# Three ring slots of the down stage loaded and split during the last quad, and two large reads cut into 256 KB pieces

## The reference

```python
def swiglu(h, w_gu, w_down):
    g, u = jnp.split(h @ w_gu, 2, axis=-1)
    return (jax.nn.silu(g) * u) @ w_down

x = x + MACARON_WEIGHT * swiglu(rms_norm(x, ffn1_norm[i]), ffn1_w_gu[i], ffn1_w_down[i])
...
x = x + MACARON_WEIGHT * swiglu(rms_norm(x, ffn2_norm[i]), ffn2_w_gu[i], ffn2_w_down[i])
gate = jax.nn.sigmoid(rms_norm(x, ple_norm[i]) @ ple_w_gate[i] + ple_b_gate[i])
e = rms_norm(p[i] @ ple_w_proj[i], ple_post_norm[i])
x = x + gate * e
```

## Time and profile before

| | us |
|---|---|
| median of three runs | 1810.19 (1809.73 to 1810.88) |
| the profiled execution, its own time | 1808.18 |
| its span, first to last instruction | 1806.1 |
| TensorE busy in it | 1706.2 (94%) |
| VectorE busy | 1290.5 (71%) |
| ScalarE busy | 694.9 (38%) |
| GpSimd busy | 296.0 (16%) |

### The profile page before, as it was taken

One profiled execution on the slowest core, in us unless ns is written; L12 is line 12 of the kernel. 1 busy time (PEld: TensorE's weight loads), 2 busy tenths in 40 slices (PEclk: granted clock), 3 DMA queues, 4 the chain that ended last, 5 costly groups with the idle time before them and its releaser, 6 DMA issues.

```text
span 1806.1 us, 20425 instructions
## 1 busy us (share of the span) xinstructions
PE 1706.2 (94%) x7314; PEld 1380.2 (76%) x7314; DVE 1290.5 (71%) x1812; ACT 694.9 (38%) x1120; POOL 296.0 (16%) x292
## 2 busy tenths in 40 slices
PE   7689999999988999999999889999999988999998
PEld 4478888888877888777777668888888866878877
DVE  7988676776644758678877799677667753666786
ACT  4343232232234435446644443223232223534442
POOL 6802221112200000024230001212221120000000
PEclk9889999999999999999899989999999989999999
DMA  7215444354377666121123214444444358776433
GB/s 280 82 43 208 169 145 166 143 181 144 125 270 254 213 217 191 57 80 47 36 76 117 82 64 146 169 154 167 163 152 158 122 181 297 226 234 189 152 121 127
DMA packets 122752, 277.69 MB, mean 154 GB/s; under 512 B 9723, under 2 KB 51356, under 8 KB 113948
## 3 DMA queue, kind: packets, MB, share of 16 engines
q1 hardware_dynamic: 115356, 263.02, 43.1%
q10 hardware_dynamic: 7296, 13.37, 2.1%
HBM read 198.23 MB, written 78.12 MB: 153 GB/s over the span
## 4 chain that ended last, share of the span: by engine, by line
PE 77%; DVE 14%; ACT 4%; issue 2%; DMA 2%; SPq 0%; ACTq 0%; DVEq 0%
PE bank L772 25%; PE bank L773 25%; PE bank L774 25%; DVE qb L1778 1%; DVE hn L1393 1%; DMA d_f<-in_wd 1%; PE bank L994 1%; DVE acc L1381 1%; ACT probs L1317 1%; DVE w_lo L1608 1%; DVE x_sb L1413 1%; DVE probs L1790 1%; DVE dn_lo L1661 1%; DVE h_lo L1425 1%; DVE rstd L1386 1%
## 5 line engine op out<-in xcount | busy, mean ns | idle before, releaser
L731 POOL TENSOR_TENSOR wdr<-wdr 128x256 f32<-128x256 f32 x176 | 165.3, 939 | 775.3 <-DMA wdr<-in_wd 765.0
L1661 DVE TENSOR_TENSOR dn_lo<-d_f,dn_hi 128x1024 fp32r<-128x1024 f32 x154 | 186.1, 1223 | 148.3 <-ACT dn_hi L1143 147.6
L772 PE MATMUL bank<-h_hi,t_hi 128*128 128x512 f32 x704 | 279.1, 396 | 6.4 <-DVE h_lo L1425 6.4
L773 PE MATMUL bank<-h_lo,t_hi 128*128 128x512 f32 x704 | 276.4, 393 | 0.0
L774 PE MATMUL bank<-h_hi,t_lo 128*128 128x512 f32 x704 | 276.0, 392 | 0.0
L772 PE MATMUL bank<-dn_hi 128*128 128x512 f32 x616 | 244.7, 397 | 29.7 <-DVE dn_lo L1661 13.9
L773 PE MATMUL bank<-dn_lo,dn_hi 128*128 128x512 f32 x616 | 242.5, 394 | 0.0
L774 PE MATMUL bank<-dn_hi,dn_lo 128*128 128x512 f32 x616 | 242.2, 393 | 0.0
L1143 ACT ACTIVATE dn_hi<-d_f 128x1024 fp32r<-128x1024 f32 x154 | 160.5, 1057 | 196.8 <-DMA d_f<-in_wd 116.7
L772 PE MATMUL bank<-c_hi,t_hi 128*128 128x512 f32 x528 | 205.4, 389 | 0.0
L773 PE MATMUL bank<-c_lo,t_hi 128*128 128x512 f32 x528 | 205.4, 389 | 0.0
(11 more groups left out here) (165 smaller groups left out, 2600.7 us busy)
## 6 DMA issues: line engine op xcount, KB each, us to landing
raw<-in_gu SPq DMA_DIRECT2D x44, 1024.0 KB, 5.7
actc<-acts SPq DMA_DIRECT2D x22, 1792.0 KB, 6.7
d_f<-actc SPq DMA_DIRECT2D x154, 256.0 KB, 3.0
raw_m<-in_units SPq DMA_DIRECT2D x52, 512.0 KB, 4.1
wdr<-in_wd SPq DMA_DIRECT2D x44, 512.0 KB, 5.4
wdc<-wdr SPq DMA_DIRECT2D x44, 512.0 KB, 3.4
d_f<-wdc SPq DMA_DIRECT2D x88, 256.0 KB, 3.2
d_f<-in_wd SPq DMA_DIRECT2D x66, 256.0 KB, 4.2
```

The source lines that it names most:

```text
L731: pool.tensor_tensor(blocks[to], blocks[one], blocks[two], ALU.add).then_inc(wd_made, 1)
L772: pe.matmul(ps, whi, vhi, start=first, stop=False, skip_group_check=onto)
L773: pe.matmul(ps, whi, vlo, start=False, stop=False, skip_group_check=onto)
L1661: dve.tensor_tensor(dn_lo[slot][:, :], d_f[slot][:, :], plain(dn_hi[slot][:, :]), ALU.subtract).then_inc(dn_split, 1)
```

## The change

Ring loads 0 to 3 move in SyncE's queue to the beginning of the last quad's round, ring load 4 between its `wd_load` and `wd_store`, and ring load 5 takes the place of ring load 2. ScalarE rounds steps 0 to 2 (`EARLY = 3`) behind `copy_p1` of the last quad, and VectorE splits them between `make_c22` and `make_c21`. The four reads of x become 16 of 256 KB, one behind each of the ring loads 12 to 27; the semaphores of x then count four pieces. The read of the per-layer input becomes eight of 256 KB, one behind each of the ring loads 45 to 52.

```diff
@@ -93,6 +93,8 @@
 STEPS = PRODUCTS * FH
 RING = 6
 STEP_INC = FH + 3
+
+EARLY = 3
 WD_AT = {P1: 0, P2: 2, Q3: 3}
 WDC_AT = {Q5: 0, Q7: 1, Q4: 2, Q6: 3}
 N_WD = 2 * FH
@@ -574,11 +576,10 @@
                 sp.dma_start(d_f[slot][:, HALF:2 * HALF].rearrange("p (h n) -> p h n", h=2),
                              weights.rearrange("h p n -> p h n")).then_inc(t2_in[slot], 16)
 
-            def x_reload(ph, i):
-                a, k = i // 2, (i % 2) * KH
+            def x_reload(ph, n):
+                a, k = n // KT, n % KT
                 src = xT if ph == 0 else x1
-                sp.dma_start(x_sb[:, k:k + KH, tok(a)],
-                             src[k * P:(k + KH) * P, tok(a)].rearrange("(k p) t -> p k t", p=P)).then_inc(x_back[i], 16)
+                sp.dma_start(x_sb[:, k, tok(a)], src[k * P:(k + 1) * P, tok(a)]).then_inc(x_back[n // KH], 16)
 
             def ffn(ph, first_units):
                 for q in (0, 1):
@@ -586,28 +587,32 @@
                     sp.wait_ge(done, value)
                     quad_load(ph, q + 2)
                 for q in range(1, QUADS):
+                    if q == QUADS - 1:
+
+                        for i in range(4):
+                            ring_load(ph, i)
                     if q % 2 == 0:
                         act_store(ph, q // 2 - 1)
                     wd_load(ph, q - 1)
+                    if q == QUADS - 1:
+                        ring_load(ph, 4)
                     wd_store(ph, q - 1)
                     if q + 3 < QUADS:
                         sp.wait_ge(t_split, t_count(ph, GU_AT[(q + 1, Q3)]))
                         quad_load(ph, q + 3)
-                ring_load(ph, 0)
-                ring_load(ph, 1)
                 wd_load(ph, N_WD - 1)
-                ring_load(ph, 2)
+                ring_load(ph, 5)
                 wd_store(ph, N_WD - 1)
-                for i in range(3, STEPS):
+                for i in range(RING, STEPS):
                     if i == RING + 1:
                         act_store(ph, FH - 1)
                     if i == FH + 1:
                         sp.wait_ge(wd_out, 16 * (ph + 1) * N_WD)
                         sp.wait_ge(act_out, 16 * (ph + 1) * FH)
                         sp.wait_ge(act_made, (ph + 1) * 2 * QUADS)
-                        for j in range(4):
-                            x_reload(ph, j)
                     ring_load(ph, i)
+                    if FH < i <= FH + 2 * KT:
+                        x_reload(ph, i - FH - 1)
                     if i >= FH + 4 and (i - FH - 4) % 4 == 0 and first_units:
                         if len(first_units) >= SLOTS:
                             sp.wait_ge(gu_made, (ph + 1) * NGU)
@@ -622,11 +627,13 @@
                         else:
                             for j in range(4):
                                 sp.wait_ge(e_out[j], 16 * (2 * KT // 4))
-                            sp.dma_start(e_sb[0][:, :, :], e_dram[0, :, 0:KT, :]).then_inc(e_in[0], 16)
                             for a in (0, 1):
                                 sp.wait_ge(re_out[a], 16)
                             sp.wait_ge(act_made, 4 * QUADS)
                             sp.dma_start(re_sb[0][:, :], e_dram[0, :, KT, :]).then_inc(re_in[0], 16)
+                    if ph == 1 and 4 * FH < i <= 4 * FH + KT:
+                        d = i - 4 * FH - 1
+                        sp.dma_start(e_sb[0][:, d, :], e_dram[0, :, d, :]).then_inc(e_in[0], 16)
 
             sp.dma_start(rel_sb[0:N_BUCKETS, :], rel).then_inc(rel_in, 16)
             sp.dma_start(oh_sb[:, :], onehot).then_inc(oh_in, 16)
@@ -1123,6 +1130,14 @@
                 act.wait_ge(c21_made, ph * QUADS + q + 1)
                 act.activation(w3[q % 2][:, :], w3[q % 2][:, :], ACT.Silu).then_inc(g1_made, 1)
 
+            def ring_round(ph, i):
+                slot, use = i % RING, ring_use(ph, i)
+                if i >= RING:
+                    act.wait_ge(dn_made, step_done(ph, i - RING))
+                act.wait_ge(s2_in[slot], 16 * use)
+                act.wait_ge(t2_in[slot], 16 * use)
+                act.activation(dn_hi[slot][:, :], d_f[slot][:, :], ACT.Copy).then_inc(dn_rounded, 1)
+
             def round_unit(n):
                 hi, _, size = unit_slot(n)
                 if slot_free(n):
@@ -1133,14 +1148,8 @@
             def down(ph):
                 na, nb = 4 * ph + 2, 4 * ph + 3
                 r = res_base(ph)
-                for i in range(STEPS):
-                    slot = i % RING
-                    if i >= RING:
-                        act.wait_ge(dn_made, step_done(ph, i - RING))
-                    use = ring_use(ph, i)
-                    act.wait_ge(s2_in[slot], 16 * use)
-                    act.wait_ge(t2_in[slot], 16 * use)
-                    act.activation(dn_hi[slot][:, :], d_f[slot][:, :], ACT.Copy).then_inc(dn_rounded, 1)
+                for i in range(EARLY, STEPS):
+                    ring_round(ph, i)
                     j, e = i // FH, i % FH
                     if j == J[P2] and e == 1:
                         for d in range(KH):
@@ -1202,6 +1211,9 @@
                     if q + 1 < QUADS:
                         for s in LOS1:
                             round_t(ph, GU_AT[(q + 1, s)])
+                    else:
+                        for i in range(EARLY):
+                            ring_round(ph, i)
                     gate0(ph, q)
                     gate1(ph, q)
                 down(ph)
@@ -1593,12 +1605,20 @@
                 make_c22(ph, q)
                 for n in todo[3:7]:
                     split_t(ph, n)
+                if not more:
+                    for i in range(EARLY):
+                        ring_split(ph, i)
                 make_c21(ph, q)
                 make_c12(ph, q)
                 gated(ph, q)
                 if q % 2:
                     mix_acts(ph, q // 2)
 
+            def ring_split(ph, i):
+                slot = i % RING
+                dve.wait_ge(dn_rounded, ph * STEPS + i + 1)
+                dve.tensor_tensor(dn_lo[slot][:, :], d_f[slot][:, :], plain(dn_hi[slot][:, :]), ALU.subtract).then_inc(dn_split, 1)
+
             def half_add(x, term, sign=1.0):
                 return dve.scalar_tensor_tensor(x, term, sign * MACARON_WEIGHT, x, ALU.mult, ALU.add)
 
@@ -1615,7 +1635,7 @@
 
                 def post_p2(d):
                     dve.wait_ge(dn_made, dn_count(ph, J[P2], FH - 1, d))
-                    dve.wait_ge(x_back[0], 16 * (ph + 1))
+                    dve.wait_ge(x_back[0], 16 * KH * (ph + 1))
                     half_add(out_tile(0, 0, d), bank2_of(P2, d)[:, :]).then_inc(res_added, 1)
 
                 def post_q6(d, i):
@@ -1626,7 +1646,7 @@
                         dve.tensor_tensor(w, bank2_of(Q6, d)[:, :], w, ALU.subtract).then_inc(w2d_made, 1)
                         return
                     dve.wait_ge(w2d_made, ph * KH + d + 1)
-                    dve.wait_ge(x_back[i], 16 * (ph + 1))
+                    dve.wait_ge(x_back[i], 16 * KH * (ph + 1))
                     a, h = [(0, 1), (1, 0), (1, 1)][i - 1]
                     sign = -1.0 if (a, h) == (1, 0) else 1.0
                     half_add(out_tile(a, h, d), w, sign).then_inc(x_step, 1)
@@ -1655,10 +1675,8 @@
                     dve.wait_ge(x_step, xs_q7(ph, d))
                     half_add(out_tile(1, 0, d), bank2_of(Q4, d)[:, :]).then_inc(res_added, 1)
 
-                for i in range(STEPS):
-                    slot = i % RING
-                    dve.wait_ge(dn_rounded, ph * STEPS + i + 1)
-                    dve.tensor_tensor(dn_lo[slot][:, :], d_f[slot][:, :], plain(dn_hi[slot][:, :]), ALU.subtract).then_inc(dn_split, 1)
+                for i in range(EARLY, STEPS):
+                    ring_split(ph, i)
                     j, e = i // FH, i % FH
                     if j == J[Q6]:
                         if e == 2:
@@ -1844,7 +1862,7 @@
                     dve.wait_ge(re_in[a], 16)
                     dve.reciprocal(re_sb[a][:, :], re_sb[a][:, :]).then_inc(e_rstd, 1)
                     dve.wait_ge(e_rstd, a + 1)
-                    dve.wait_ge(e_in[a], 16)
+                    dve.wait_ge(e_in[a], 16 * (KT, 1)[a])
                 link(dve.scalar_tensor_tensor(e, e, col(C_G["post"] + d), re_sb[a][:, :], ALU.mult, ALU.mult))
                 dve.wait_ge(sig_made, m + 1)
                 link(dve.tensor_tensor(e, e, sig[m % 2][:, :], ALU.mult))
```

## The result

The changed kernel takes 1786.38 us (median of four runs, 1782.53 to 1789.44), the kernel before 1810.54 on the same chip: a ratio of 0.9866 (95% interval 0.9854 to 0.9879), 24 us faster. Forecast were 1773.0 and a range of 1769.5 to 1781. The profiled execution is the slowest of the four, 1789.44 us.

A forecast was written before the change was run, and what follows sets the result against it. TensorE was taken as the bound nearly everywhere. 1808.2 less 37.5 us of removed stalls gave 1770.7, 1771.0 with 0.3 for step 7, and 1773.0 against the median; range 1769.5 to 1781.

The forecast's parts named there:

- The five terms of the gain: Stalls removed: early loads and splits 8.3 and 9.9 us, x in pieces 8.0 and 8.75, per-layer input 2.6; together 37.5.
- ScalarE's and VectorE's early work: Last quad: roundings of 3.2 us inside 10.28 idle, splits of 3.7 inside 4.75 idle; cost nothing.
- Step 3: Down stage: its split, still behind the mixes, has 1.9 and 1.2 us to spare; cost zero.
- the DMAs of steps 12 to 27: Down stage: ring loads, x pieces and units need 337 GB/s against 397 seen; queue 85% full, cost zero.
- SyncE's queue: Around the down stage's start: reordered loads and stores still serve steps 6 and 7 in time; 0.3 us in all.
- the term for steps 6 and 7: Start of both down stages: step 7 has 1.6 and 0.8 us to spare; 0.3 us taken in all.
- rival A: Down stage: step 3 or 7 misses TensorE beyond its spare; +5 or +10 us, time 1775 to 1783; chance 0.15.
- B: Steps 12 to 27 saturate DMA, noticed by TensorE from about 268 GB/s down; 1777 to 1793 us; chance 0.08.
- C: Small DMAs of steps 12 to 27 and 45 to 52 cost the queue fixed time; 1870 us; chance 0.03.
- D: Last quad: ring loads 0 to 3 stay late and the first split stays where it is; 1791 us; chance 0.04.

The follow-up runs named there:

- both_moves: Changed kernel with load 20 of the down weights ahead of ring loads 0 to 3 and last store of weight sums behind ring load 7; 1769.32 us.
- pieces_only: Kernel before with only the pieces of x and of the per-layer input, none of the early loads and splits; 1788.84 us.
- store_mid: Changed kernel with the last store of weight sums behind ring load 6, ahead of the store of activations and ring load 7; 1786.51 us.

## Why the prediction was wrong

**Right.** The five terms of the gain, 37.5 us. With the new waits taken out, a profiled execution took 1770.89 us (`both_moves`) against 1808.18, 37.3 less. They are right part by part too: the terms say 16.3 us for the first block and 21.25 for the second with the per-layer input, and the table shows 16.6 (735.2 to 718.6) and 21.4 (232.3 to 210.9). By medians `both_moves` gains 41.6 us, 4 more than the terms, and lies 3.7 us under the forecast of 1773.0: the two profiled executions lie 2.8 us under and 1.6 us over the medians they belong to, and no run tells why. ScalarE's and VectorE's early work fits into the idle time, though VectorE's with less room than costed: its three splits took 4.58 us and not 3.7, beside POOL's sums, and end 0.26 us before `make_c21` begins (504.89). Step 3 is in time, and the DMAs of steps 12 to 27 hold up nobody: the rates of 256 KB ring loads carried over to the pieces. On this the Trainium skill's rule of at least 1 MiB a DMA ("DMA: Bandwidth & Descriptors", section Bandwidth) would have led the other way; the trace decides against it for transfers queued behind each other. The fit that the prediction took from that page is given there for DMAs issued from GpSimd, and these are issued by SyncE.

**The step that failed** is "SyncE's queue", in three places. First, "The last `wdc` store, at 509.05, so moves by 0 to 5.6 us": it moved by 7.6, to 516.68. I counted the issue of four ring loads, which made load 20 only 1.9 us later, but not that this load lands behind their 2.1 MB (POOL's data 7.0 us after the issue and not 4.1), nor that VectorE's splits and mixes slow POOL's sums from 3.2 to 5.1 and 5.8 us. I had noted the slower VectorE beside POOL and not turned it round. The Trainium skill has the rule ("GPSIMD Engine Reference", section Key points: GpSimd shares its SBUF interfaces with VectorE, with contention when VectorE has two SBUF inputs); the traces agree, 3.18 us without such splits and 4.9 to 5.8 with them. Second, "The store may now go as soon as the mixes are done, about 512.8": it stands behind ring load 6, and that behind the `wdc` store, so it went at 518.8. The text gave ring load 6 an issue of up to 514.7 a few sentences earlier and then let its successor go before it. Third, the spare for step 6 (rounded and split by 524.1, issued by 514.7) did not hold, since ring load 6 went at 517.3. With these, the term for steps 6 and 7, put at 0.3 us in all, measured 15.0 in the profiled execution: 8.8 us idle in the four waits and nearly all of the rest at the lower clock behind three of them.

The mechanism of **rival A** is what happened, at a chance of 0.15, but A named steps 3 and 7 and not step 6. It was priced at 5 to 10 us, with one stall of up to 2.4 us in a block; there are two in each, 0.8 and 3.6, 2.6 and 1.8, and the clock fell behind three of the four. That is 15.0 us in the two down stages, and 3.5 us in the part with the mixer came on top of it in this execution. By medians the change lost 17.1 us against `both_moves`, of which 13.4 show against the forecast, because that lay 3.7 above `both_moves`: the two misses partly cancel, by luck.

**Rivals B, C and D** did not occur: no wait between steps 11 and 44 in `pieces_only`, the pieces lost nothing, and step 0 had no wait. The range ended at 1781 because it took in A's lower part only; A's own time, 1775 to 1783, ended below the 1786.4 measured too.

## What to carry to other kernels

When a DMA is moved forward in a queue that also waits for other engines, follow every later entry of that queue by its program order, and add up what stands behind each waiting entry: here a store that the queue itself asks for only at step 12 stood ahead of the loads of steps 6 and 7, and its place cost 15 us. A transfer that others wait for goes ahead of one that waits. Large reads cut into pieces and spread one per step cost nothing here, where all transfers together came to 307 to 319 GB/s and backed-up ring loads had shown 397. Work moved into idle time of VectorE slowed GpSimd beside it.

## What was not expected of the hardware

- POOL's four sums of 128x256 took 3.18 to 3.19 us alone and 4.9 to 5.8 beside VectorE's subtractions of two SBUF tiles, 6.1 in the worst round; the mixes of VectorE took 4.09 instead of 2.6 beside them.
- After a stall of TensorE the clock sometimes falls and sometimes not: behind waits of 3.6, 2.6 and 1.8 us in the changed kernel it fell to 0.50 of full speed (1.2 GHz) for 3 to 4 us, behind 2.4 us in the kernel before and 2.7 us in `store_mid` (529.5 to 534.5) it stayed at 1.00. The part with the mixer, with nearly the same waits, took 740.2 to 746.5 us. The Trainium skill ("TensorE: Matmul & The Clock Gate", section Part 1) says that the gate's timing does not start with the kernel, and that the same kernel therefore has more or fewer slow matmuls at its start from run to run; the scatter of the changed kernel, 7 us over four runs, would fit that, but no run here separates it.
